# Last stage of a two-layer streaming encoder: TensorE's four lowest levels and the cross scores put behind the old rows' transposes, and both gates put ahead of the levels' copies

## The reference, cut to what matters

```python
def hgrn2_block(S, q, k, i, log_f):
    A = jnp.cumsum(log_f, axis=1)
    decay = jnp.exp(where(causal, A[:, :, None] - A[:, None, :], -inf))
    attn = einsum('bthk,btshk,bshk->bhts', q, decay, k)
    o = einsum('bhts,bshv->bthv', attn, i) + einsum('bthk,bhkv->bthv', q * exp(A), S)
    S_new = exp(A[:, -1])[..., None] * S + einsum('bshk,bshv->bhkv', k * exp(A[:, -1:] - A), i)
    return S_new, o
# then: o = rmsnorm(o, g);  y = concat(o, cross_attn(xq, mk, mv)) * silu(gate);  x = x + y @ w_out;  rmsnorm(x, final_g)
```

## Time and profile before

| what | us |
|---|---|
| median of 3 runs (lowest, highest) | 2396.69 (2394.6, 2402.66) |
| the profiled execution's own time | 2400.24 |
| its span, first to last instruction | 2398.5 |
| TensorE busy (matmul) | 2316.5, 97% |
| VectorE, ScalarE, GpSimd busy | 1821.9, 1417.4, 379.6 |
| mean granted TensorE clock, as a share of full speed | 0.991 |

### The profile page before, as it was taken

How to read it: one execution, slowest core, us unless ns; L and a number is a source line. 1 busy time by engine, 2 the same in 40 slices (tenths; PEclk the granted TensorE clock), 3 DMA queues, 4 the chain that set the end, 5 groups by cost and what they waited for, 6 DMA issues and landing times. The chain is left out here.

```text
span 2398.5 us, 61540 instructions
## 1 busy us (share of the span) xinstructions
PE 2316.5 (97%) x23701; PEld 2099.2 (88%) x23701; DVE 1821.9 (76%) x3555; ACT 1417.4 (59%) x3281; POOL 379.6 (16%) x585
## 2 busy tenths in 40 slices
PE   8999999999989999999998999999999989999998
PEld 5999999999867888888887999999999968788886
DVE  7899787887666656656666998797878777788885
ACT  4564666755555555555554564766757566666664
POOL 2332000000022111111112331000000112112111
PEclk9999999999999999999999999999999989999999
DMA  6886987879893222222325887887879693443442
GB/s 234 295 294 229 299 281 221 253 226 324 234 294 98 86 88 72 82 65 82 90 87 209 278 293 240 268 260 217 261 242 304 222 270 103 129 141 121 135 135 69
DMA packets 396663, 469.62 MB, mean 196 GB/s; under 512 B 39860, under 2 KB 248556, under 8 KB 396376
## 3 DMA queue, kind: packets, MB, share of 16 engines
q1 hardware_dynamic: 379832, 406.02, 54.0%
q0 software_dynamic: 14704, 54.92, 6.6%
q10 hardware_dynamic: 1840, 4.75, 0.8%
HBM read 318.77 MB, written 151.56 MB: 196 GB/s over the span
## 5 line engine op out<-in xcount | busy, mean ns | idle before, releaser
L1460 PE MATMUL pj_acc<-x_hi,pj_wh 128*128 128x256 f32 (+1 forms) x3080 | 785.2, 285 | 0.0
L1460 PE MATMUL pj_acc<-x_lo,pj_wh 128*128 128x256 f32 (+1 forms) x3080 | 785.1, 285 | 0.0
L1460 PEld LDWEIGHTS pj_acc<-x_lo,pj_wh 128*128 128x128 f32 x3080 | 579.4, 188 | 0.0
L1460 PEld LDWEIGHTS pj_acc<-x_hi,pj_wh 128*128 128x128 f32 x3080 | 579.4, 188 | 0.0
L503 ACT ACTIVATE pj_wh<-pj_wt 128x512 fp32r<-128x512 f32 x676 | 420.3, 634 | 259.6 <-DMA pj_wt<-tsum 182.1
L510 DVE SCALAR_TENSOR_TENSOR pj_wl<-pj_wt,pj_wh 128x512 fp32r<-128x512 f32 x676 | 468.8, 710 | 88.2 <-ACT pj_wh L503 83.4
L1456 PE MATMUL pj_acc<-x_hi,pj_wl 128*128 128x256 f32 (+1 forms) x3080 | 512.4, 288 | 13.7 <-DVE pj_wl L510 11.9
L1456 PEld LDWEIGHTS pj_acc<-x_hi,pj_wl 128*128 128x128 f32 x3080 | 427.8, 188 | 22.2 <-DVE pj_wl L510 19.5
L1301 DVE TENSOR_TENSOR pj_out<-pj_out,pj_acc 128x512 f32<-128x512 f32 (+1 forms) x448 | 320.3, 715 | 108.1 <-PE pj_acc L1460 74.3
L2520 DVE COPY pb_pt<-pb_SCTP 128x256 f32<-128x256 f32 (+2 forms) x266 | 115.7, 435 | 154.8 <-PE pb_SCTP L2338 79.8
L2655 ACT ACTIVATE pb_se<-pb_se,pb_mn 128x640 f32<-128x640 f32 (+4 forms) x208 | 154.6, 745 | 117.6 <-DVE pb_mn L2503 117.3
(11 more groups left out here) (354 smaller groups left out, 3938.9 us busy)
## 6 DMA issues: line engine op xcount, KB each, us to landing
pj_wt<-tsum SPq DMA_DIRECT2D x546, 256.0 KB, 3.8
proj<-pj_out SPq DMA_DIRECT2D x112, 512.0 KB, 4.2
tsum<-pj_wt SPq DMA_DIRECT2D x140, 256.0 KB, 3.0
pj_wraw<-in_w_in_dram POOLq DMA_DIRECT2D x24, 1024.0 KB, 6.5
tsum<-pj_wraw SPq DMA_DIRECT2D x56, 256.0 KB, 4.2
hg_x<-x_mid SPq DMA_DIRECT2D x17, 512.0 KB, 3.6
pb_gate<-proj SPq DMA_DIRECT2D x16, 512.0 KB, 5.1
pb_x<-in_x_prompt_dram SPq DMA_DIRECT2D x16, 512.0 KB, 3.5
```

The costliest lines, as they stand in the source:

```text
L1460: ins = nc.tensor.matmul(BANK[j][:, 0:n], w.hi[j][:, k], x.of(y, p, j)[:, k], start=False, stop=(k == 3 and i == 1))
```

## The change

For tiles with t > 0, TensorE does the rest of the late chunks and both `turn_outputs` directly behind `turn_values`, and then levels 0 to 3 and the cross scores in one run. VectorE does both gates directly behind the norms, then places 0 to 2, the second `add`, place 3, and only then the first low part, the two minima and the second low part. The turn of the banks becomes 0, 1, 2, 3, x0, x1, kv0, kv1, 4, 5, 6, 7. Tile 0 keeps its order. No instruction is added or removed.

```diff
--- before.py
+++ after.py
@@ -2814,7 +2814,8 @@
         def order_of(t):
 
             kv = [("kv", 0), ("kv", 1)] if t else []
-            return [0, 1, 2, ("x", 0), ("x", 1), 3] + kv + [4, 5, 6, 7]
+            near_of = [0, 1, 2, 3, ("x", 0), ("x", 1)] if t else [0, 1, 2, ("x", 0), ("x", 1), 3]
+            return near_of + kv + [4, 5, 6, 7]
 
         place_of = {}
         owner = []
@@ -3097,22 +3098,22 @@
                     if t:
                         project(t - 1, LATE, LATE + 2)
                         turn_values(t)
-                        level(t, 0)
-                        level(t, 1)
+                        project(t - 1, LATE + 2, LATE + 4)
+                        turn_outputs(t, 0)
+                        project(t - 1, LATE + 4, CHUNKS)
+                        turn_outputs(t, 1)
+                        for i in (0, 1, 2, 3):
+                            level(t, i)
+                        cross_scores(t)
                     else:
                         level(0, 0)
                         turn_outputs(0, 0)
                         turn_outputs(0, 1)
                         level(0, 1)
                         turn_values(0)
-                    level(t, 2)
-                    if t:
-                        turn_outputs(t, 0)
-                        project(t - 1, LATE + 2, LATE + 4)
-                        turn_outputs(t, 1)
-                        project(t - 1, LATE + 4, CHUNKS)
-                    cross_scores(t)
-                    level(t, 3)
+                        level(0, 2)
+                        cross_scores(0)
+                        level(0, 3)
                     project(t, 0, 3)
                     if t:
                         update(t - 1, 0)
@@ -3274,22 +3275,28 @@
                         norm(t - 1, 0)
                         mean(t - 1, 1)
                         norm(t - 1, 1)
-                    place(t, 0)
-                    place(t, 1)
-                    if t:
                         gate(t, 0)
-                    place(t, 2)
-                    low_part(t, 0)
-                    if t:
                         gate(t, 1)
+                        place(t, 0)
+                        place(t, 1)
+                        place(t, 2)
                         add(t - 1, 1)
-                    low_part(t, 1)
-                    if t == 0:
+                        place(t, 3)
+                        low_part(t, 0)
+                        least(t, 0)
+                        least(t, 1)
+                        low_part(t, 1)
+                    else:
+                        place(0, 0)
+                        place(0, 1)
+                        place(0, 2)
+                        low_part(0, 0)
+                        low_part(0, 1)
                         for r in Next.LATE_ROWS:
                             weights_low(r)
-                    least(t, 0)
-                    least(t, 1)
-                    place(t, 3)
+                        least(0, 0)
+                        least(0, 1)
+                        place(0, 3)
                     step(t, 3)
                     if t:
                         state(t - 1, 0)
```

## The result

The change made the kernel slower by about 1%. Six runs each: 2399.01 us before (2394.6 to 2402.66), 2421.78 us after (2415.65 to 2427.05); the ratio is 1.01, with its 95% interval from 1.0085 to 1.0115. That is 22.8 us. I had forecast 2405.5 with a range up to 2417: the direction was right, the size was not. The profiled span is 2418.7 us against 2398.5.

A forecast was written before the change was run, and what follows sets the result against it. TensorE, 97% busy, bounds the kernel, with code supply a second limit. Holes +14.2, clock +2, old holes -6, update's wait -2: together +8, from 2400.24 to 2408; allowing for the median, +9 to 2396.69 gives 2405.5, range 2394 to 2417.

The forecast's parts named there:

- TensorE's order: Last stage's tiles: level 0 at +3.5, levels done at +5.5, cross scores done at +6.57 against +6.77; no instruction added.
- banks: Score banks: level 3 takes the first update's, first cross scores the second's; exponentials end by +9.1 against its +10.4.
- VectorE's order: Gates before places: third place ends about +5.65, so cross scores start at +5.7, 0.2 behind the levels, projection at +6.8.
- The wait of 0.31: First state update waits for the cross scores' exponentials; 0.31 us in an undisturbed tile, 0.27 net gain when it goes.
- Code: In the run of levels 0 to 3 TensorE uses up instructions before the next q8 packet is usable: holes, +14.2 us.
- the code is hidden: Rival: instruction fetch causes no loss in the run, only the update's wait goes; 2394 or 2389 us, chance 0.15 plus 0.05.
- fewer or shorter holes: Rival: packets asked for earlier than estimated, or slipping in between the loads; +2 to +5, 2400 us, chance 0.20.
- how often: Share of tiles with a hole in the run: asks in 122 of 250 places are bad, 7 to 8 of 15 tiles.
- How long: Length of each hole in the run: TensorE dry from +5.2 to +5.5, packet usable at +7.3; 1.8 to 2.1, say 1.9 us.
- Clock, +2: TensorE at 1.2 GHz after holes: one or two stretches in all, some 1.5 us each, +2 us.
- Every hole costs its clock: Rival: six more stretches at the lower clock, 1.5 us each; 2414 us, chance 0.12.
- Queues: SyncE's query load comes 0.65 us later with gate and tile loads; data first needed at +17.5, so covered, no cost.

The follow-up runs named there:

- the two repeats kernels: Changed kernel and kernel before, each with 14 level 4 matmuls repeated in tiles 1 to 15 and 44 in tile 0: 2392.58 and 2395.74 us.
- repeat_early: Changed kernel with 14 level 4 matmuls issued twice in tiles 1 to 15 and 30 repeated matmuls in tile 0: 2447.22 us, ratio 1.0212.
- turn_only: Kernel before with only level 3 ahead of the cross scores, the bank turn to suit, place 3 ahead of the minima: 2405.16 us, ratio 1.0032.
- repeat_hole: Changed kernel with 14 level 4 matmuls issued twice in tiles 1 to 15 and 8 of level 0's in tile 0: 2468.94 us, ratio 1.0295.
- repeat_safe: Changed kernel with 14 level 4 matmuls issued twice in tiles 1 to 15 and 44 of level 0's in tile 0: 2392.58 us, ratio 0.9985.

## Why the prediction was right or wrong

- **TensorE's order, banks, VectorE's order: right.** In tiles without a hole all starts came within 0.05 us of the forecast (+3.50, +5.75, +6.81, +9.02), the cross scores 0.21 behind the levels, the tile at 25.05 to 25.15. The wait of 0.31 went; what that is worth in 14 tiles, some 3.6 us, is in the traces of the two repeats kernels.
- **The mechanism of Code: right.** The holes stand in the run or just behind, no engine ends them, and a q8 packet lands in each of the ten (in the eleventh case 0.5 us ahead of the idle time, 1.5 before work goes on). The rivals "the code is hidden" and "fewer or shorter holes" fell. So did the rule of the Trainium skill ("Runtime: NRT & Kernel Launch", "Instruction fetch mechanics") that TensorE stores 2048 instructions and the fetch is mostly hidden: repeat_early ran dry in every tile at the end of a packet of 256.
- **The term that failed is "how often", 7.5 x 1.9 = 14.2.** I took a store of 320 instructions at the moment of asking, and from that a bad zone of 122 of 250 places, half of the tiles. Measured are between 84 and 99 places of 128: ten tiles, and an eleventh behind the cross scores. In matmuls of the run my zone is the places 139 to 200, and the seven tiles that lie in it all had their hole, 14.7 us in all, as forecast. The miss is the lower edge: the holes after 118, 130 and 134, 8.0 us, where by a store of 320 the packet would have been asked for ahead of the tile and come in time. It started at +4.8 to +5.2, behind the loads. With the 1.1 us of the eleventh, at place 201, these are 9.1 us. The two holes that I had to go by the earlier trace rows gave a lower bound in that one place, 275 instructions issued after the packet began, and I made an average store of it.
- **"How long" was low by less:** 1.9 against 2.1 in the seven tiles of my zone and 22.7 / 10 = 2.3 in all ten. Packets started at about +5, as I had said, but the earliest place runs dry at +4.8, not +5.2, and work went on up to 1.6 us behind a packet, where I had 1.35. "How often" and "how long" together gave 23.8 instead of 14.2, which is 9.6 us of the miss.
- **Clock, +2:** four stretches, 5.7 us, where the one before cost some 1.5. "Every hole costs its clock" was too dark (4 of 10 did), and my +2 too light. Its price of 1.5 per stretch held (1.0 to 1.6).
- **Queues, "Covered": wrong.** The load has time, but the packet for levels 4 to 7 comes later with it, as far as the one tile of turn_only above tells. In the whole change this is small: 3.7 us at these levels and just behind in 14 tiles, against 2.9 before.
- **The range** ended at 2417 because its worst case had eight holes; with ten of 2.3 and four stretches of clock my own sum would have given 23.8 + 5.7 - 6 - 2 = +21.5, against +20.2 in the spans. The parts were right and two counts were not.

## What to carry to other kernels

A kernel whose engine is busy 97% of its span can still be bound by how fast its code comes, and a stretch of small matmuls is where that shows. Before packing dense pieces into one run, count instructions per microsecond there, and look in the trace for idle time on "issue" with an instruction packet inside it. Then judge a reordering by its undisturbed tiles and by its holes separately, since the holes also move when nothing but the number of instructions ahead changes; a few repeated instructions are a cheap way to tell the two apart.

## What the runs showed of the hardware that I had not expected

- The place of the code alone moved this kernel by 76 us, 3% (repeat_hole and repeat_safe).
- An instruction packet of 16 KB takes 1.0 to 1.4 us in the ten holes of the kernel after, and TensorE goes on 1.3 to 1.6 us after it has landed.
- How far ahead a packet comes has a bound. Put the packets' ends every 256 instructions from where the holes stand, and count over the last stage of all fourteen traces: none of its 811 packets starts more than 288 instructions ahead of its own first instruction. A store of 320 when the packet is asked for would show some 312 where TensorE is slow (a projection matmul and its weight load take 0.24 us, so the 1 us of my step is some 8 instructions). Where it is slow a packet can start ahead of the entry to the packet before. In the kernel after, the code behind place 105 was on its way 1.7 us ahead of its tile (2035.91), where TensorE entered the packet before at +0.0. The code behind place 118, whose packet before is entered at +1.8, when the loads come, didn't start within the first 5.0 us (2171.65, above). The DMA queues from 2034.1 to 2034.4:

```profile
q8 instruction: 1, 0.02, 19.7%
```

The trace doesn't show the asking itself, so what sets it stays open, and the 256 above is what to count on, not a law.
- Four of ten holes of 1.8 to 2.9 us had 3.4 us at half clock begin at their end or within 1.6 us of it, and six hadn't. What separates them stayed open: a hole of 1.76 us had one, one of 2.54 had none.
